# Seven block products (Strassen's scheme) in place of eight in the conv stage of a fused transformer layer

## What is computed

```
proj = h @ w_in                      # h: 640 x 1024
bg, cg, u_in, ..., g_conv, g_mla     # each 1024 columns of proj
u = pad(cg * u_in)
conv = u[:-2]*w[0] + u[1:-1]*w[1] + u[2:]*w[2]
y_conv = (bg * conv) @ w_conv_out
merged = sigmoid(g_conv) * y_conv + sigmoid(g_mla) * (attention @ w_o)
x = x + gate1 * (merged @ w_mix_out)
x = x + gate2 * HierMoE(rmsnorm(x) * (1 + scale2) + shift2)   # 32 experts
```

## Time and profile before

| what | value |
|---|---|
| median of 3 executions | 918.02 us |
| profiled execution, first to last instruction (span) | 916.3 us |
| PE busy | 874.4 us (95%) |
| DVE busy | 421.8 us (46%) |
| ACT busy | 276.0 us (30%) |
| POOL busy | 110.5 us (12%) |
| granted TensorE clock, mean | 0.988 |
| data moved | 198.86 MB |

### The profile page before, as it was taken

One profiled execution on the slowest core, in us unless ns is written; L12 is line 12 of the kernel. 1 busy time (PEld: TensorE's weight loads), 2 busy tenths in 40 slices (PEclk: granted clock), 3 DMA queues, 4 the chain that ended last, 5 costly groups with the idle time before them and its releaser, 6 DMA issues. The chain is left out here.

```text
span 916.3 us, 15131 instructions
## 1 busy us (share of the span) xinstructions
PE 874.4 (95%) x6078; PEld 694.8 (76%) x6078; DVE 421.8 (46%) x907; ACT 276.0 (30%) x522; POOL 110.5 (12%) x123
## 2 busy tenths in 40 slices
PE   5999999999999999999999999993999999999996
PEld 4787777888899999999999998882555555555551
DVE  3667355555444252433513195368443443434333
ACT  5357654655411212112122132333111111111123
POOL 0000000000000000000000040201223333332320
PEclk9999999999999999999999999996899999999999
DMA  9972624602313222122141148669899999999948
GB/s 333 352 289 99 242 107 161 209 23 69 107 47 92 60 77 92 46 92 92 46 161 46 47 152 249 186 266 354 348 415 415 416 414 415 413 414 417 414 163 343
DMA packets 73681, 198.86 MB, mean 217 GB/s; under 512 B 11384, under 2 KB 43112, under 8 KB 61080
## 3 DMA queue, kind: packets, MB, share of 16 engines
q1 hardware_dynamic: 65800, 181.71, 53.8%
q0 software_dynamic: 7824, 16.36, 4.8%
HBM read 189.30 MB, written 18.17 MB: 226 GB/s over the span
## 5 line engine op out<-in xcount | busy, mean ns | idle before, releaser
L819 PE MATMUL pair<-w_ug,xgT 128*64 128x256 f32 x1184 | 138.1, 386 | 1.3 <-ACT xgT L956 1.3
L1748 ACT CAST hi<-raw 128x2048 fp32r<-128x2048 f32 (+3 forms) x31 | 53.8, 1735 | 224.8 <-PE pair L1356 202.1
L1352 PE MATMUL pair<-hT,hi 128*128 128x320 f32 x512 | 116.8, 309 | 0.0
L1356 PE MATMUL pair<-hT,lo 128*128 128x320 f32 x512 | 116.7, 309 | 0.0
L1354 PE MATMUL pair<-hT,hi 128*128 128x320 f32 x512 | 116.6, 309 | 0.0
L819 PEld LDWEIGHTS pair<-w_ug,xgT 128*64 128x64 f32 x1184 | 84.7, 139 | 42.0 <-issue 4.4
L1930 DVE TENSOR_TENSOR lo<-raw,hi 128x2048 fp32r<-128x2048 f32 (+2 forms) x30 | 65.6, 2188 | 109.2 <-ACT hi L1748 108.4
L1352 PEld LDWEIGHTS pair<-hT,hi 128*128 128x128 f32 x512 | 85.7, 188 | 0.2 <-issue 0.2
L1354 PEld LDWEIGHTS pair<-hT,hi 128*128 128x128 f32 x512 | 85.6, 188 | 0.0
L1356 PEld LDWEIGHTS pair<-hT,lo 128*128 128x128 f32 x512 | 85.5, 188 | 0.0
L838 PE MATMUL pair<-w_dn,actT 128*64 128x512 f32 x296 | 71.7, 605 | 1.3 <-issue 0.9
(11 more groups left out here) (355 smaller groups left out, 1474.2 us busy)
## 6 DMA issues: line engine op xcount, KB each, us to landing
w_ug<-in_w_up SPq DMA_DIRECT2D x32, 1024.0 KB
w_ug<-in_w_gate SPq DMA_DIRECT2D x32, 1024.0 KB
w_dn<-in_w_down SPq DMA_DIRECT2D x32, 1024.0 KB
raw<-in_w_in SPq DMA_DIRECT2D x20, 1024.0 KB, 5.3
ada_a<-in_w_ada SPq DMA_DIRECT2D x14, 1024.0 KB, 12.1
raw<-in_w_ada SPq DMA_DIRECT2D x10, 1024.0 KB, 5.7
ya<-expert_rows SPq DMA_DIRECT2D x5, 1024.0 KB, 9.0
raw<-in_w_conv_out SPq DMA_DIRECT2D x4, 1024.0 KB, 5.0
```

Source lines behind the costliest of these rows:

```text
L819: x = pe.matmul(bank[2 + d % 2][g * SL:(g + 1) * SL, 0:DE], xgT[d % 2][:, k, h * SL:(h + 1) * SL], w_ug[r][:, g, h, k, :], start=(n == 0), ...
L1352: pe.matmul(o, st[0], m[0], start=first, stop=False)
L1356: x = pe.matmul(o, st[1], m[0], start=False, stop=last)
L1748: act.copy(hi[n % 2][:, 0:size], raw[n % 4][:, 0:size]).then_inc(hi_done, 1)
```

## The change

The conv stage becomes 16 products, one for each of the four blocks and each pair of column tiles (j, j + 4). One such product (640 tokens x 1024 features times 1024 x 256) is seen as 2 x 2 blocks: A11, A12, A21, A22 are the token halves by the feature halves of h, B11 to B22 the feature halves by the two column tiles of w. Instead of eight block products seven are made, on sums of blocks, and the results are combined. A block product, a "unit", is 4 feature tiles x 3 matmuls of 320 columns = 12 matmuls. The loop `Fori` is gone; 112 units are written out.

- The row sums (d_sum 0 to 3, sums of blocks of h) are made by POOL during the attention, 20 instructions of 128x640, in three groups between the stores of g_mla chunks; ACT and DVE split them.
- The weight sums are made by DMAs that add: POOL issues a DMA that reads a 512 x 128 block of w_in from DRAM and adds it onto the block in SBUF (256 KB, in runs of 512 B). Each product has four (kinds 0 to 3). Q_SUM holds in turn B11+B12, then +B22, then +B21, and Q_B22 becomes B22+B12. Kind 1 waits until unit 1 is split, kind 2 until unit 3 is, kind 3 until unit 4 is, since they overwrite what those read; units 4, 5 and 6 are cast from what they leave.
- SP loads each product as 512 KB plus two blocks of 256 KB again, into one of three `raw` tiles.
- ACT casts unit g + 6 (`unit_hi`) and DVE splits unit g + 5 (`unit_lo`) at step g. Units 2 and 3 accumulate on top of units 0 and 1 in PSUM, so PE waits at unit 2 until ACT has copied the first product (`p1_s`), and at unit 3 for the copy `v_s`.
- DVE combines the products: first_sum, second_sum, last_sums.
- At the end of the attention PE makes unit 0 before the last transposes. Some semaphores are merged.

```diff
+    UAHEAD = 6
+    unit_turn = {31 + g: g for g in range(4)}
+    sum_turn = {35: 0, 36: 1, 37: 2}
+    UNIT_SRC = (Q_B11, Q_SUM, Q_B21, Q_B22, Q_SUM, Q_B22, Q_SUM)
+    UNIT_SUM = (None, 0, None, None, 1, 2, 3)
...
@@ SP @@
-        with sp.Fori(0, 4) as it:
-            for q, c0 in enumerate((C_CG, C_U, C_BG, C_GC)):
-                load(N_CONV + q, kpc(w_in[:, bass.ds(it * 256 + c0, 256)]), KD, 256, it, 4)
+        for i in range(NPROD):
+            it, x, _, _ = product_of(i)
+            if i < 3:
+                sp.wait_ge(lo_done, N_GM + i + 1)
+            else:
+                sp.wait_ge(s_ulo, 7 * (i - 2))
+            dst = raw[i % 3]
...
@@ POOL @@
+        def row_sum(n):
+
+            dst, x, y, less = SUMS[n]
+            for h in range(2):
+                ks = slice(2 * h, 2 * h + 2)
+                if n:
+                    pool.wait_ge(pchain, 2 * n - 1 + h)
+                op = pool.tensor_sub if less else pool.tensor_add
+                op(dst[:, ks, :], x[:, ks, :], y[:, ks, :]).then_inc(pchain, 1)
+
+        def w_sum(kind, i):
+
+            if kind == 0:
+                pool.wait_ge(raw_in[i % 3], conv_in_count(i))
+            else:
+                pool.wait_ge(s_ulo, 7 * i + (None, 2, 4, 5)[kind])
+            q = Q_B22 if kind == 2 else Q_SUM
+            kh, nh = ((0, 1), (1, 1), (0, 1), (1, 0))[kind]
+            pool.dma_start(raw[i % 3][:, q].rearrange("p (k c) -> p k c", k=4), w_quarter(i, kh, nh),
+                           accum_op=ALU.add).then_inc(sum_done(kind, i)[0], 16)
...
+        w_sum(3, 0)
+        for i in range(1, NPROD):
+            if i + 1 < NPROD:
+                w_sum(0, i + 1)
+            for kind in range(1, 4):
+                w_sum(kind, i)
...
@@ PE @@
+        def conv_product(g):
+
+            i, m = divmod(g, 7)
+            pe.wait_ge(s_ulo, g + 1)
...
+            if m == 2:
+                pe.wait_ge(s_pcopy, 2 * i + 1)
+            if m == 3:
+                pe.wait_ge(s_pcopy, 2 * i + 2)
...
+            for k in range(4):
+                x = prod(out, [t[:, k * P:(k + 1) * P] for t in w], [t[:, k, :] for t in rows],
+                         k == 0 and m not in (2, 3), k == 3, adds=m in (2, 3))
+            x.then_inc(s_pu, 1)
...
@@ ACT @@
+        def unit_hi(g):
+
+            i, m = divmod(g, 7)
+            if m == 0:
+                act.wait_ge(raw_in[i % 3], conv_in_count(i))
+            elif UNIT_SUM[m] is not None:
+                act.wait_ge(*sum_done(UNIT_SUM[m], i))
+            if g >= 8:
+                act.wait_ge(s_pu, g - 7)
+            else:
+                act.wait_ge(piece_used, N_GM + 3 + g // 4)
+            act.copy(unit_w(g)[0], unit_src(g)).then_inc(s_uhi, 1)
...
+        for g in range(UNITS):
+            i, m = divmod(g, 7)
+            it, x, j, j4 = product_of(i)
+            if m == 1:
+                act.wait_ge(s_pu, 7 * i + 1)
+                if i >= 2:
+                    act.wait_ge(s_comb, combined(i - 2, BLKS))
+                act.copy(p1_s[i % 2][:, :], prod_bank(i, 0)).then_inc(s_pcopy, 1)
+            if m == 2:
+                act.wait_ge(s_pu, 7 * i + 2)
+                act.copy(v_s[i % 2][:, :], prod_bank(i, 1)).then_inc(s_pcopy, 1)
+            if g + UAHEAD < UNITS:
+                unit_hi(g + UAHEAD)
...
@@ DVE @@
+        for g in range(UNITS):
+            i, m = divmod(g, 7)
+            x = i % 4
+            if g + UAHEAD - 1 < UNITS:
+                unit_lo(g + UAHEAD - 1)
+            if m == 0 and i:
+                last_sums(i - 1)
+            if x == BG and m in (1, 2):
+                if m == 1:
+                    dve.wait_ge(s_comb, combined(i - 1, BLKS))
+                    tap(0, i)
+                    tap(1, i)
+                else:
+                    tap(2, i)
...
```

More of the change, by code:

```diff
@@ L193, in build @@
     mixer = ExitStack()
-    raw = [sb(f"raw{i}", [P, PIECE], scope=mixer) for i in range(4)]
+    raw = [sb(f"raw{i}", [P, PIECE], scope=mixer) for i in range(3)]
+    in_raw3 = ExitStack()
+    u = [sb(f"u{i}", [P, T + 4], scope=in_raw3) for i in range(2)]
+    p1_s, v_s = ([sb(f"{n}0", [P, HALF], scope=in_raw3)] for n in ("p1_s", "v_s"))
+    in_raw3.close()
+    raw.append(sb("raw3", [P, PIECE], scope=mixer))
     hi, lo = [], []
@@ L396, in build @@
     y_out = [sem(f"y_out{i}") for i in range(2)]
[L397 removed]
+    s_yt = sem("yt_rdy")
     def v3(t, k, c):
@@ L1342, in _, with prod @@
     def _(pe):
-        def prod(out, st, mv, first, last):
-            pe.matmul(out, st[0], mv[0], start=first, stop=False)
-            pe.matmul(out, st[0], mv[1], start=False, stop=False)
-            return pe.matmul(out, st[1], mv[0], start=False, stop=last)
+        def prod(out, st, mv, first, last, adds=False):
+            pe.matmul(out, st[0], mv[0], start=first, stop=False, skip_group_check=adds)
+            pe.matmul(out, st[0], mv[1], start=False, stop=False, skip_group_check=adds)
+            return pe.matmul(out, st[1], mv[0], start=False, stop=last, skip_group_check=adds)
         def prod2(outs, st, mvs, first, last):
@@ L2210, in _, with c_of, times @@
-        base[:] = 0, 0
-        links[0] = l0 + 4 * LINKS_CONV
+                x = dve.memset(t[:, a:a + (2 if a == 513 else 1)], 0.0)
+        link(x)
+        def c_of(j, a, z):
+            return conv[j][:, a:z]
+        U11 = (0, HALF, 1),
+        U2 = (HALF, N_SAMPLE, HALF + 1), (N_SAMPLE, T, N_SAMPLE + 3)
+        def times(x, j, src, a, spans_):
+            if x == UU:
+                for z0, z1, at in spans_:
+                    y = dve.tensor_mul(u[j // 4][:, at:at + z1 - z0], src[:, z0 - a:z1 - a], c_of(j, z0, z1))
+                return y
+            return dve.tensor_mul(c_of(j, a, a + HALF), src, c_of(j, a, a + HALF))
@@ new lines, in last_sums @@
+        def last_sums(i):
+            it, x, j, j4 = product_of(i)
+            p1, v = p1_s[i % 2][:, :], v_s[i % 2][:, :]
+            dve.wait_ge(s_pcopy, 2 * i + 2)
+            dve.wait_ge(s_comb, combined(i, SECOND_N))
+            if x in (CG, GC):
+                d21, d22 = ((c_of(b, HALF, T) if x == CG else merged[b][:, HALF:T]) for b in (j, j4))
+                dve.wait_ge(s_pu, 7 * i + 7)
+                dve.tensor_sub(d21, prod_bank(i, 4), p1).then_inc(s_comb, 1)
+                dve.tensor_add(d22, p1, v).then_inc(s_comb, 1)
+                return
+            link(dve.tensor_add(v, p1, v))
+            dve.wait_ge(s_pu, 7 * i + 7)
+            dve.tensor_sub(p1, prod_bank(i, 4), p1).then_inc(s_comb, 1)
+            times(x, j4, v, HALF, U2)
+            dve.wait_ge(s_comb, combined(i, BLK21))
+            times(x, j, p1, HALF, U2).then_inc(s_comb, 1)
@@ new lines, in tap @@
+        def tap(n, i):
+            _, _, j, j4 = product_of(i)
+            for b in (j, j4):
+                w = vT[:, 24 + 8 * n + b:25 + 8 * n + b]
+                for a, z, at in ((0, N_SAMPLE, n), (N_SAMPLE, T, N_SAMPLE + 2 + n)):
+                    out, src = c_of(b, a, z), u[b // 4][:, at:at + z - a]
+                    if n == 0:
+                        x = dve.tensor_scalar(out, src, w, None, ALU.mult)
+                    else:
+                        x = dve.scalar_tensor_tensor(out=out, in0=src, scalar=w, in1=out, op0=ALU.mult, op1=ALU.add)
+            link(x)
@@ L2213, in _ @@
+        last_sums(NPROD - 1)
+        conv_lo(6)
+        conv_lo(7)
+        split_lo(N_G + 1, PIECE)
         for mp in range(4):
```

502 lines of the change are left out of this document (329 added, 173 removed).

## The result

The changed kernel takes 982.21 us in the median of 4 runs (979.96 to 985.52), beside 918.11 us (917.73 to 918.52) of the kernel before on the same chip: a ratio of 1.070, 95% interval 1.067 to 1.072. It is 64 us slower. The forecast was 940 us with a range of 897 to 976: the sign was right, the time lies above the range.

A forecast was written before the change was run, and what follows sets the result against it. PE alone was taken to bound the kernel; with fewer matmuls, landings of adding DMAs would set the conv stage's pace. +18 us for the stage and +4 for the attention on 918.0 gave 940 us, range 897 to 976.

The forecast's parts named there:

- the attention, "+4": Attention: POOL's row sums delay stores, ACT's copy of chunk 13 comes 5 us late, costing PE about 4 us.
- 20 t - 33: Attention: lateness in us of ACT's copy of chunk 13, t being one POOL addition, 1.67 to 2.3, taken as 1.9.
- S: Conv stage: L1 + L3, the two adding-DMA landings in the loop of waits, taken as 9 us.
- 5.2 + S: Conv stage: period in us of the loop of waits per product, against 12.3 that PE needs.
- L1: Conv stage: landing of the kind 1 weight sum, beside SP's load of a later product, taken as 5.0 us.
- L3: Conv stage: landing of the kind 3 weight sum, taken as 4.0 us from the median of POOL's gathers.
- 104 + 16 S: Stretch from the unit-38 transposes to the conv stage's end, landings setting the pace, taps included: 248 us forecast.
- The taps: Conv stage: bg's 12 tap instructions on DVE delay unit 1's split by about 4 us, four times: 16 us.
- The break-even at S = 7.6: Whole kernel: with the attention's 4 us, the changed kernel equals the one before at this S; slower from there on.
- The first rival: Conv stage: landings of 2.4 to 3.5 us are hidden, PE sets the pace; 898 us, up to 910; chance 0.33.
- The clock: Conv stage: waits of 2 to 6 us per product may bring back PE's lower clock; 0 to 15 us, slow cases only.
- Rival with 988 us: Conv stage: adding transfers cost twice and load the engines, S = 12, stretch 296 us; chance 0.20 for over 964.

The follow-up runs named there:

- run 2: Changed kernel with each POOL row sum waiting for the one just ahead of it, in the same three groups: 961.88 us, ratio 1.048.
- run 1: Changed kernel with the 20 row sums spread over units 21 to 34 of the attention: 960.49 us, ratio 1.047.
- run 3: Changed kernel with all adding DMAs (weight sums) left out: 929.02 us, 15 of them from other tokens behind the stretch; stretch 201.9 us.
- Run 5: Changed kernel with the 12 tap instructions of a bg product spread over its seven places on DVE: 967.78 us, ratio 1.054.
- run 7: Changed kernel with its 64 adding DMAs as plain copies of the same bytes, so no sums are made: 966.82 us, 15 from other tokens.

## Why the prediction was wrong

**The step that failed: the attention, "+4".** Its price was the row sums' own time, passed on by the late stores (20 t - 33), with "DVE's work with operands in SBUF ... stretches them". It was the other way round. POOL was not stretched, t was 1.52 (a lower end of 1.67 was forecast), and so the stores were hardly late; DVE was held, over a whole run of sums, and with it PE. The mechanism stood in the text as a sentence on the port: each normalisation held "for up to an addition", 1 to 2 us in all, and left out of the sum. The runs put it at 20.5 to 21.5 us (runs 2 and 1 against the changed kernel), out of 25.4. Had the attention cost 4 us, the kernel would have taken about 961 (run 1), inside the range. That runs 1 and 2 keep 3.9 and 5.0 us there is near the forecast's 4 by luck, since no late store is in it.

The rows before did not show this. At the earlier trace rows a second subtraction follows the first at once (533.74 to 535.31, then from 535.28), and DVE still had its turn between them: its split ended at 536.40, and the second subtraction took 2.56 us in place of 1.57. Why there and not among the row sums is open. Back to back alone does not decide it.

**The stage: right mechanism, its term too small.** PE's part was all but exact: 202.6 forecast, 201.9 in run 3. The loop was right: the idle time is at unit 2, for p1_s, behind ACT's waits for landings. The period too: from the wait at 276.13 to that at 521.35 lie 15 periods; the four with bg are 19.4 us long, the eleven others 15.2. With S = 10 the forecast's 5.2 + S is 15.2, and 4 more behind bg is 19.2. Both rows:

```profile
276.13 0.38 PE L1518 MATMUL pair<-hT,hi 128*128 128x320 f32 x1 [4.96 <-ACT p_s L2159]
...
521.35 0.61 PE L1518 MATMUL pair<-hT,hi 128*128 128x320 f32 x1 [6.53 <-ACT p_s L2159]
```

**The landing.** L1 was taken as 5.0 and L3, after POOL's gathers, as 4.0; they were 5.3 and 4.7 in the mean. S was 10 and not 9: 16 of the 20 us by which the stage was missed. By 104 + 16 S it is 264; 268.4 was measured. The upper bound of 4.9, made from packets, was nearer than the chosen row. The estimate of 2.6 us by the Trainium skill (DMA: Bandwidth & Descriptors, Anatomy of one DMA) does not agree: even the plain ones took 3.3 at least here, so the measurement decides against it for this transfer with its rows of 512 B.

**The taps.** 16 us were forecast. With bg the way from the cast of unit 1 to the end of its split takes 6.13 us in place of 1.35, so 4.8 us four times, 19 in all. Run 5 leaves 1.3 of each 4.8 and gave back 13.7. With S = 10 and 19 for the taps the formula is at 267.

**The break-even at S = 7.6.** No run tested it. Plain transfers bring S to 8.0 only, and a stretch above the 230 us of the kernel before is what the formula says there, though 242 is 10 more than its 232. The first rival, "hidden" at 898, needed S under 7.1, and even plain copies do not come to that.

**The clock.** It was given to the slow cases alone, "0 to 15 us". It cost 17.5 us of matmul time in the stage. Since landings and taps alone account for 267 of the 268.4, nearly all of that lay inside the landings' period.

**Rival with 988 us.** Its cause, engines loaded with twice the packets, was there (2.3 us of all engines per adding DMA, DMA share 0.77), but S stayed at 10. That the time came near it was the attention's doing.

## What to carry to other kernels

A run of instructions on GpSimd, back to back, can shut VectorE out for the whole run: let each wait for its predecessor, or place them one by one where VectorE is not due. When a wait shows a late copy, look for the first late thing on that engine's queue: moving the copy brought 2 us, moving the sums off the DMA queue 39. And a loop over transfers is to be priced with the landings of just those transfers, beside what runs at their time, and not with one median over all of them.

## What the runs showed of the hardware

- A DVE tensor_scalar of 128x128 was held for 23.24 us beside 16 back-to-back POOL instructions (and across a 0.55 us DMA issue among them); with a wait between each two, a gap of 0.08 us, the same one took 0.30 us and the longest hold was 1.79 us. Between two subtractions of POOL (533.74 and 535.28 of the kernel before), with no gap in the record, a DVE split did get its turn.
- The forms held were tensor_scalar and tensor_tensor with operands in SBUF; DVE's reductions from PSUM took 0.82 us beside the sums of run 2 as elsewhere. In run 2 each held one ended 0.09 to 0.55 us, by its form, behind the end of a sum; where a sum ended soon after its start, as with the one of 0.30 us, no hold is to be seen.
- A DMA of 256 KB that adds into SBUF in rows of 512 B lands after 4.7 us, or 5.3 where it mostly runs beside loads; it takes POOL 1.28 us to issue, 528 packets and 2.3 us of all 16 engines. For a plain one of the same bytes and shape (run 7) it is 3.4 or 4.6 us, 0.75 us, 80 packets and 0.9 us.
